# SSD exponents from one 32-row matmul per head and direction, in a hybrid SSD, MLA and GLA encoder on one core

## The reference, cut to what matters

```python
def step(state, inp):                       # ssd_scan, one chunk of 128 tokens
    xc, dtc, bc, cc = inp
    acum = jnp.cumsum(dtc * a, axis=1)
    diff = acum[:, :, None] - acum[:, None, :]
    decay = jnp.exp(jnp.where(causal, diff, -jnp.inf))
    cb = jnp.einsum('blgn,bsgn->blsg', cc, bc)
    scores = cb[..., None] * decay * dtc[:, None]
    y = jnp.einsum('blsge,bsgep->blgep', scores, xc)
    y = y + jnp.einsum('blgn,bgepn->blgep', cc, state) * jnp.exp(acum)[..., None]
    ...
y_fwd = ssd_scan(xs, dt[:, :, 0], a[0], b_in, c_in)
y_bwd = flip_seq(ssd_scan(flip_seq(xs), flip_seq(dt[:, :, 1]), a[1], flip_seq(b_in), flip_seq(c_in)))
y = y_fwd + y_bwd + xs * d_skip.astype(f32).reshape(SSD_GROUPS, SSD_HPG)[:, :, None]
```

## Time and profile before

| | |
|---|---|
| median of 3 runs | 1332.7 us (1330.87 to 1333.67) |
| the profiled execution, its own time | 1333.24 us |
| its span, first to last instruction | 1331.4 us |
| PE busy | 1316.7 us (99% of the span) |
| DVE, ACT, POOL busy | 770.4, 642.1, 624.0 us |
| mean granted clock of TensorE | 0.996 |
| input projection | to 155 us |
| SSD heads on PE behind it | 155 to 195 us |
| attention, first layer | 197 to 285 us |

### The profile page before, as it was taken

The page is one execution under the profiler, slowest core; times in us unless marked ns, Lnnn a source line. Parts: engine busy times, 40 slices in busy tenths (PEclk is TensorE's granted clock), DMA queues, the critical chain, the costliest instruction groups (busy, mean ns, idle before and its releaser), DMA issues.

```text
span 1331.4 us, 16274 instructions
## 1 busy us (share of the span) xinstructions
PE 1316.7 (99%) x6540; PEld 1112.0 (84%) x6540; DVE 770.4 (58%) x842; ACT 642.1 (48%) x1029; POOL 624.0 (47%) x294
## 2 busy tenths in 40 slices
PE   9999999999999999999999999999999999999997
PEld 7878878888898888888889988888998888888887
DVE  5857486840079998885000863436379988882002
ACT  6654777652355544444223586555555444443221
POOL 3344461245524654445553354755535644445551
PEclk9999999999999999999999999999999999999998
DMA  5342111123223333333332323311223333333331
GB/s 207 96 119 80 53 35 41 64 80 96 83 92 95 95 99 102 100 92 87 103 90 89 124 64 95 95 60 65 83 96 97 101 102 97 95 89 96 93 87 64
DMA packets 41147, 119.77 MB, mean 90 GB/s; under 512 B 4592, under 2 KB 11632, under 8 KB 41072
## 3 DMA queue, kind: packets, MB, share of 16 engines
q1 hardware_dynamic: 39712, 116.43, 28.5%
q10 hardware_dynamic: 1360, 2.29, 0.6%
HBM read 116.35 MB, written 2.23 MB: 89 GB/s over the span
## 4 chain that ended last, share of the span: by engine, by line
PE 92%; DVE 5%; ACT 1%; SPq 1%; DMA 0%; issue 0%; ACTq 0%; DVEq 0%
PE bank L345 26%; PE bank L349 26%; PE bank L348 26%; DVE sqacc L674 1%; PE bank L1819 1%; PE bank L1817 1%; PE bank L1818 1%; PE bank L2057 1%; PE bank L1370 1%; PE bank L1550 1%; PE bank L1553 1%; PE bank L398 1%; PE bank L2039 1%; PE bank L1337 1%; PE bank L1580 1%; PE bank L1339 1%
## 5 line engine op out<-in xcount | busy, mean ns | idle before, releaser
L318 POOL TENSOR_TENSOR wlo<-raw,whi 128x1024 fp32r<-128x1024 f32 (+2 forms) x214 | 530.9, 2494 | 621.5 <-ACT whi L312 621.4
L345 PE MATMUL bank<-xw_hi,whi 128*128 128x512 f32 (+1 forms) x1272 | 474.9, 374 | 1.6 <-DVE xw_lo L734 0.9
L349 PE MATMUL bank<-xw_hi,wlo 128*128 128x512 f32 (+1 forms) x1256 | 466.8, 372 | 0.0
L348 PE MATMUL bank<-xw_lo,whi 128*128 128x512 f32 (+1 forms) x1256 | 466.7, 372 | 0.0
L312 ACT ACTIVATE whi<-raw 128x1024 fp32r<-128x1024 f32 (+2 forms) x215 | 219.7, 1025 | 206.0 <-DMA raw<-in_fout 112.6
L345 PEld LDWEIGHTS bank<-xw_hi,whi 128*128 128x128 f32 x1272 | 239.7, 188 | 44.2 <-issue 2.1
L349 PEld LDWEIGHTS bank<-xw_hi,wlo 128*128 128x128 f32 x1256 | 236.5, 188 | 41.6
L348 PEld LDWEIGHTS bank<-xw_lo,whi 128*128 128x128 f32 x1256 | 236.7, 188 | 40.2 <-issue 0.2
L607 DVE RECIPROCAL small<-small 128x2 f32<-128x2 f32 x8 | 1.3, 164 | 315.2 <-ACT small L532 313.9
L760 DVE SCALAR_TENSOR_TENSOR cbuf<-ubuf,par,cbuf 128x510 f32<-128x510 f32 x100 | 168.8, 1688 | 3.5
L345 PE MATMUL bank<-g_hi,whi 128*128 128x512 f32 (+1 forms) x396 | 145.3, 367 | 0.2
(11 more groups left out here) (282 smaller groups left out, 1458.8 us busy)
## 6 DMA issues: line engine op xcount, KB each, us to landing
raw<-in_fin SPq DMA_DIRECT2D x88, 512.0 KB, 3.6
raw<-in_fout SPq DMA_DIRECT2D x32, 448.0 KB, 3.3
raw<-in_gin SPq DMA_DIRECT2D x25, 512.0 KB, 3.6
raw<-in_hin SPq DMA_DIRECT2D x22, 512.0 KB, 3.7
raw<-in_hout SPq DMA_DIRECT2D x16, 512.0 KB, 3.7
raw<-in_fout SPq DMA_DIRECT2D x16, 512.0 KB, 3.5
raw<-in_gout SPq DMA_DIRECT2D x8, 512.0 KB, 3.7
xres<-in_x SPq DMA_DIRECT2D x8, 256.0 KB, 4.6
```

Source lines behind the costliest of these rows:

```text
L318: engine.tensor_tensor(wlo[s][:, 0:n], raw[s][:, 0:n], whi[s][:, 0:n].bitcast(F32), ALU.subtract).then_inc(w_lo, 1)
L345: first = nc.tensor.matmul(out_ap, wh, ah, start=start, stop=False)
L348: nc.tensor.matmul(out_ap, wh, al, start=False, stop=False)
L349: return first, nc.tensor.matmul(out_ap, wl, ah, start=False, stop=stop)
```

## The change

The masks by -2^30 and the bias of the exponentials go away. Instead the whole exponent of a head and direction comes from one matmul over 32 rows: eight rows hold the high part of a_l of eight heads and eight the low part (`moving`, 512 columns), with ones for the head that is picked in the stationary tile, and 16 rows hold u_s, high and low, for four blocks in the stationary tile (`steady`), with ones for the block in `moving`. Rows 0 to 31 and 32 to 63 are the two directions of heads 0 to 7, rows 64 to 127 those of heads 8 to 15. The tables are made in three steps: DVE splits a_f and u_f in high and low rows (two operations more), SP writes them to DRAM (4 DMAs) and reads them back in place (16 DMAs) between the loads of blocks 10 to 14, and ACT fills the constant parts.

The two directions are joined before the exponential: DVE copies the backward exponent over the forward one where s > l (`copy_predicated`), then ACT takes one exponential of 128x512. The diagonal has the forward weight alone; the backward diagonal and the skip are a per-token coefficient (`coef`), made from sums of B times C (POOL, two products; PE, eight matmuls of one column; DVE, two small operations). POOL (chunks 0 to 3) and DVE (chunks 4 to 7) multiply x by it, token by channel, and PE adds it to the near product by four matmuls with the identity per chunk. wx[1] moves from POOL to DVE, into the first four heads. `skip` goes away. The far and near parts are summed in `reach`, so SP's next load of `reach` waits for `gated` of two chunks before, where it waited for DVE's far part.

```diff
@@ pe_spread @@
-            v = n % 2
             if first:
-                pe.wait_ge(sem("picks"), 4)
-                pe.wait_ge(sem("dt_dve"), 11)
-                pe.wait_ge(sem("at_in"), 16)
+                pe.wait_ge(sem("decays_in"), 4 * 4 * 16)
+                pe.wait_ge(sem("coef"), 1)
             else:
-                pe.wait_ge(sem("ssd_both"), n - 1)
+                pe.wait_ge(sem("ssd_exp"), n - 1)
             for d in range(2):
-                pick = ident_r[:, 32 * d + n:32 * d + n + 1].to_broadcast([P, P])
-                nc.tensor.matmul(abank(v, d)[:].rearrange("p (b x) -> p b x", b=NBLK), never_r[:, d * P:(d + 1) * P],
-                                 eye_r[:].unsqueeze(1).broadcast_to([P, NBLK, P]), start=True, stop=False)
-                nc.tensor.matmul(abank(v, d)[:], pick, at_both[:], start=False, stop=True).then_inc(sem("a_mm"), 1)
+                rows = slice(32 * (2 * (n // GHEADS) + d), 32 * (2 * (n // GHEADS) + d + 1))
+                j = n % GHEADS
+                nc.tensor.matmul(abank(n, d)[:], steady[rows, j * P:(j + 1) * P], moving[rows, :], start=True,
+                                 stop=True).then_inc(sem("a_mm"), 1)
@@ joining and exponentials @@
-        def dve_both_ways(dve, n):
-
-            dve.wait_ge(sem("ssd_exp"), EXPS * (n + 1))
-            nc.vector.tensor_tensor(ebuf[n % 4][:], ebuf[n % 4][:], abank(n, 1)[:], ALU.add).then_inc(
-                sem("ssd_both"), 1)
+        def dve_either_way(dve, n):
+
+            dve.wait_ge(sem("a_mm"), 2 * n + 2)
...
+            nc.vector.copy_predicated(fore, mask, back).then_inc(sem("ssd_way"), 1)
...
-            for b in range(NBLK):
-                at = slice(b * P, (b + 1) * P)
-                nc.scalar.activation(ebuf[n % 4][:, at], abank(n, 0)[:, at], ACT.Exp, bias=u_s(b, 0)).then_inc(
-                    sem("ssd_exp"), 1)
-            act.wait_ge(sem("a_mm"), 2 * n + 2)
-            for b in range(NBLK):
-                o = abank(n, 1)[:, b * P:(b + 1) * P]
-                nc.scalar.activation(o, o, ACT.Exp, bias=u_s(b, 1)).then_inc(sem("ssd_exp"), 1)
+            nc.scalar.activation(ebuf[n % 4][:], abank(n, 0)[:], ACT.Exp).then_inc(sem("ssd_exp"), 1)
@@ dve_ssd @@
-                nc.vector.tensor_tensor(bank[6][:], bank[6][:], reach[c % 2][:], ALU.mult).then_inc(sem("ssd_far"), 1)
-
-            def skip(c):
...
+                nc.vector.tensor_tensor(reach[c % 2][:], bank[6][:], reach[c % 2][:], ALU.mult).then_inc(
+                    sem("ssd_far"), 1)
...
                 if n + 2 < HEADS:
-                    dve_both_ways(dve, n + 2)
-                if n % 2:
-                    skip(c)
-                elif n:
+                    dve_either_way(dve, n + 2)
+                if n and n % 2 == 0:
                     gated(c - 1)
+                if n < NBLK:
+                    dve_late_x(dve, n)
@@ dve_late_x @@
+            nc.vector.tensor_tensor(by_head(wx[1], i), by_head(xtok[1], i), far_weight(i, 1), ALU.mult).then_inc(
+                sem("wx_late"), 1)
+            nc.vector.tensor_tensor(own_part(4 + i), own_x(4 + i), own_coef(4 + i), ALU.mult).then_inc(
+                sem("own_dve"), 1)
@@ y(n) of pe_ssd @@
+                if u == 0:
+                    pe.wait_ge(sem("own_dve" if c >= 4 else "own_pool"), c % 4 + 1)
+                    for b in range(NBLK):
+                        at = slice(b * P, (b + 1) * P)
+                        nc.tensor.matmul(bank[4 + c % 2][:, at], ck(xbc, c)[:, at], ident[:], start=b == 0,
+                                         stop=False)
@@ pe_own_sums, behind block 20 @@
+            for b in range(NBLK):
+                for g in range(2):
+                    last = nc.tensor.matmul(bank[2][:, 2 * b + g:2 * b + g + 1], ebuf[2 + g][:, b * P:(b + 1) * P],
+                                            ones[:, 0:1], start=True, stop=True)
@@ dve_dt @@
+            step(nc.vector.tensor_copy(rows_of[2][:], u_f))
+            done(13)
+            step(nc.vector.tensor_tensor(rows_of[3][:], u_f, rows_of[2][:].bitcast(F32), ALU.subtract))
@@ block.sync @@
+                if f == BASE["hin"] + 10:
+                    sp_decays_out(sp)
+                if 0 <= f - BASE["hin"] - 11 < 4:
+                    sp_decays_in(sp, f - BASE["hin"] - 11)
@@ sp_reach @@
             if c >= 2:
-                sp.wait_ge(sem("ssd_far"), c - 1)
+                sp.wait_ge(sem("ssd_y"), 2 * c - 2)
```

More of the change, by code:

```diff
@@ L194, in build_program @@
             ebuf = [sb(f"ebuf{i}", T, F32, s) for i in range(4)]
+            with ExitStack() as q:
+                rows_of = [sb(f"rows{i}", T, F32R, q, 64) for i in range(4)]
             cbm = sb("cbm", 4 * T, F32, s)
-            at_both = sb("at_both", T, F32R, s)
-            at_lo = sb("at_lo", T, F32R, s, 64)
+            moving = sb("moving", T, F32R, s)
             reach = [sb(f"reach{i}", T, F32, s) for i in range(2)]
             gt = sb("gt", T, F32, s, 64)
-            ident_r = sb("ident_r", 64, F32R, s)
-            eye_r = sb("eye_r", P, F32R, s)
-            never_r = sb("never_r", 2 * P, F32R, s)
             cols = sb("cols", NBLK * 2 * 64, F32, s)
+            steady = sb("steady", GHEADS * P, F32R, s)
+            coef = sb("coef", NBLK * HEADS, F32, s)
         with ExitStack() as s:
@@ L990, in pool_hin @@
                 los(pool, at)
+                if at == BASE["hin"] + TURN0:
+                    pool_b_times_c(pool)
             pool.wait_ge(sem("cb_set"), NBLK)
+            for c in range(KD // 2):
+                pool_own(pool, c)
             pool_mask(pool, 0)
@@ L1109, in pe_dt_turn @@
             for b in range(NBLK):
-                for w, src in enumerate((w_f, u_f)):
+                for w, src in enumerate((w_f, dt_f)):
                     last = nc.tensor.transpose(bank[2][:, b * P + w * 64:b * P + w * 64 + 64],
@@ new lines, in pe_own_sums, with dve_coefs @@
+        def pe_own_sums(pe):
+            pe.wait_ge(sem("b_times_c"), 2)
+            pe.wait_ge(sem("dt_dve"), 15)
+            for b in range(NBLK):
+                for g in range(2):
+                    last = nc.tensor.matmul(bank[2][:, 2 * b + g:2 * b + g + 1], ebuf[2 + g][:, b * P:(b + 1) * P],
+                                            ones[:, 0:1], start=True, stop=True)
+            last.then_inc(sem("own_sums"), 1)
+        def dve_coefs(dve):
+            dve.wait_ge(sem("own_sums"), 1)
+            backward = cols[:].rearrange("p (b x) -> p b x", b=NBLK)[:, :, 96:96 + HEADS]
+            nc.vector.tensor_tensor(coef[:].rearrange("p (b g n) -> p b g n", b=NBLK, g=2),
+                                    backward.rearrange("p b (g n) -> p b g n", g=2),
+                                    bank[2][:, 0:2 * NBLK].rearrange("p (b g) -> p b g", b=NBLK).unsqueeze(3).broadcast_to(
+                                        [P, NBLK, 2, GHEADS]), ALU.mult).then_inc(sem("coef"), 1)
+            dve.wait_ge(sem("coef"), 1)
+            every = coef[:].rearrange("p (b n) -> p b n", b=NBLK)
+            nc.vector.tensor_tensor(every, every, con("skips", HEADS).unsqueeze(1).broadcast_to([P, NBLK, HEADS]),
+                                    ALU.add).then_inc(sem("coef"), 1)
@@ L1204, in abank @@
             return bank[2 * (1 - n % 2) + d]
-        def dve_both_ways(dve, n):
-            dve.wait_ge(sem("ssd_exp"), EXPS * (n + 1))
-            nc.vector.tensor_tensor(ebuf[n % 4][:], ebuf[n % 4][:], abank(n, 1)[:], ALU.add).then_inc(
-                sem("ssd_both"), 1)
+        def dve_either_way(dve, n):
+            dve.wait_ge(sem("a_mm"), 2 * n + 2)
+            mask = con("later").bitcast(mybir.dt.uint32).unsqueeze(1).broadcast_to([P, NBLK, P])
+            fore, back = (abank(n, d)[:].rearrange("p (b l) -> p b l", b=NBLK) for d in range(2))
+            nc.vector.copy_predicated(fore, mask, back).then_inc(sem("ssd_way"), 1)
         def dve_ssd(dve):
@@ L2493 @@
     cst, rope, glac = _constants()
+    cst[:, CCOLS["skips"]:CCOLS["skips"] + HEADS] = np.asarray(inputs["ssd_d"])[0]
     data |= {"cst": cst, "rope": rope, "glac": glac}
```

127 lines of the change are left out of this document (79 added, 48 removed).

## The result

The changed kernel takes 1334.17 us (median of 20 runs, 1333.19 to 1335.80); the kernel before, run beside it on the same chip, 1331.80 (20 runs, 1330.03 to 1334.22). The ratio is 1.0017, 95% interval 1.0011 to 1.0024: 2.3 us slower, 1.5 to 3.2. That is the "no difference" of the forecast, which drew its line at 0.2%, and 0.7 from its 1333.5. But the forecast had set a change of +0.8 on a median of 1332.7 from three runs; over 20 runs that median is 1331.8, and the change +2.4. So 1.6 us of the change are to be explained, and the hit in the number is partly luck.

A forecast was written before the change was run, and what follows sets the result against it. PE's own list of work bounds the kernel, with ACT, DVE and POOL following. Terms summed to +0.8 on the profiled 1333.24, giving 1334.0, or 1333.5 us as the median; range 1329.8 to 1337.8, one in ten on each side.

The forecast's parts named there:

- no difference: Whole kernel: time within 0.2% (2.7 us) of the kernel before; chance 0.54.
- spreads, with the shape changes: SSD heads on PE: two matmuls for four in 16 heads, -9.3, and 12 changes of array shape, +1.8.
- identity matmuls: SSD chunks on PE: four float32 matmuls of 128 columns per chunk, not hidden, 8 x 0.87 = +7.0.
- sums of B times C: PE's list: eight matmuls of one column with the start of the next block, +1.8; POOL's and DVE's parts hidden.
- block 11: Block 11 starts late through two new DVE operations in the table chain, +0.9 (ends 0 and 2.0).
- wait at head 5: Start of the heads: PE waits for head 3's exponential, behind head 2's joining, exponential and ACT's table loads; +1.8.
- clock behind it: Rival: the clock falls in the new wait at head 5, the stage pays up to 1.6, 1335.1; chance 0.08.
- end of the stage: End of the heads: PE's idle time of 1.97 shrinks to 0 to 0.45, -1.6.
- clock at `rope(0)`: Half clock at 197 to 200 us behind the 1.97 idle goes with PE busy up to `rope(0)`, -1.6.
- no overlap: Rival: the two directions' spread matmuls do not overlap, as shape changes could drain the array; +1.9, 1335.4; chance 0.13.
- DVE's backlog: First two chunks: DVE needs 5.6 against PE's 5.0, largely inside PE's wait; 0.3 at most, not booked.
- the DVE rival: Rival: joining of 1.2 to 1.4 makes DVE hold PE in the first two chunks, 1336.7 or 1338; chance 0.17.

The follow-up runs named there:

- the last experiment: The kernel with three repairs (ACT's detour, DVE's late operations, decay rows moved), with B times C taken from the diagonal of cbm; 1328.73 us, ratio to the kernel before 0.9976.
- the joining twice: The changed kernel with each head's copy_predicated done twice, the second waiting for the first; 1338.73 us in its one run.
- the detour moved: The changed kernel with block 22's silu, the next high part and both ACT table loads ahead of head 2's exponential; 1332.46 us, ratio to the kernel before 1.0006.
- load 10: The changed kernel with SP's load of block 10 ahead of the decay-row writes, and the reads one load later; 1333.87 us, ratio 1.0011.

## Why the forecast was right or wrong

Each term beside what the traces show. "Measured" is the shift between the same PE instructions in the two profiled executions, or the piece itself.

| step | forecast | measured | from |
|---|---|---|---|
| spreads, with the shape changes | -7.5 | -8.7 | heads 0 to 3 0.39 each, the others 0.6 (1.19 per chunk) |
| identity matmuls | +7.0 | +7.1 | 8 x 0.89 |
| sums of B times C | +1.8 | +1.8 | 1.68 and 0.11 at the next block's start; 1.83 in the last experiment |
| block 11 | +0.9 | +1.4 | wait 1.17, and a first matmul of 0.47 |
| wait at head 5 | +1.8 | +1.8 | 1.81 |
| clock behind it | rival, 0.08 | +1.6 | only in some executions; it covers 0.7 of DVE's backlog |
| end of the stage | -1.6 | -1.6 | 1.97 to 0.38 |
| closing sums | 0 | -0.1 | before, L1385 waited 0.13 for DVE's L1221 |
| clock at `rope(0)` | -1.6 | -1.5 | in one of the two executions of the kernel before |
| sum | +0.8 | +1.8 | up to `rope(0)` |
| outside the span | 0 | +0.3 | 2.1 in each of 20 runs, 1.8 before |

**The mechanisms** came out nearly all as said: PE's list sets the time, the eight identity matmuls are not hidden, the exponentials that ACT lost are worth nothing, the wait at head 5 has the cause, place and length that were worked out, and a joining of double length has the price that its rival gave it.

**The spread** is the term that was mis-sized. I took the middle between side by side and one after the other, 0.34 for a pair, from the near products, whose overlap in columns is partial. The pair in different rows overlaps entirely: 0.23, beside the 0.20 of its change of shape. The changes of shape were sized too low in turn, 0.15 each where the chain shows 0.20. So 16 x (0.92 - 0.23) is -11.0 for the -9.3, and 12 x 0.20 is +2.4 for the +1.8. The forecast had named the Trainium skill, TensorE: Matmul & The Clock Gate, Part 3; the trace agrees with it (4 ns, and 0.23 less per pair than in one row group). With the other page of the Trainium skill that it had named, TensorEngine Tiling (Array Packing), Key Properties, the traces agree as far as a change costs something, and the price stands beside the overlap, not in its place: 0.20 for the change back to 128 rows. The rival "no overlap" fell. With the pair and the changes right the sum would have been about -0.3, further from the +2.4 of the medians: this error and the next ones partly hid each other.

**Block 11** was named with its causes and sized too low. DVE's two operations cost the 1.0 that was worked out. SP's order, whose cover the forecast called thin, cost 0.2, and the first matmul behind the wait 0.2.

**The clock** was a wrong kind of term. I read a half clock behind one idle time in one execution as its consequence, and booked 1.6 for its going. It is a chance, in the kernel before as in the new one, and the new wait has one too (four of six traces). Booking the one in full and leaving the other as a rival of 0.08 put the forecast 1.6 low against these two executions. How often each falls over many runs isn't known.

**DVE's backlog** at the start was put at 0.3 at most and not booked. It is 0.73 where the clock stays up. The step that failed: I let the backlog lie in PE's wait, but two operations that read two SBUF tiles waited out a POOL mask each there (timelines of the changed kernel):

```profile
163.97 1.75 DVE L1263 TENSOR_TENSOR wx<-xtok,cols 128x512 f32<-128x512 f32 x1
165.64 1.75 DVE L1265 TENSOR_TENSOR xbc<-xtok,coef 128x512 f32<-128x512 f32 x1
163.62 3.23 POOL L1202 TENSOR_TENSOR ebuf<-ebuf,cbm 128x512 f32<-128x512 f32 x2
```

Each started just behind a mask (163.62 and 165.13) and ended 0.55 behind its end (165.17 and 166.85).

**The joining** "has no row" is wrong: the kernel before has COPY_PREDICATED in its second layer, which I had passed over, in the groups of DVE:

```profile
L2206 DVE COPY_PREDICATED att<-tri,bank 128x256 f32<-128x256 uint32 x8 | 3.1, 442 | 3.5 <-PE bank L2039 3.5
```

442 ns for 256 columns. The new one takes 686 for 512. With that row the DVE rival would not have held 0.17.

**Outside the span** 0.3 us were added in every run. What makes them isn't settled; no run was made for it. The kernel with the joining twice had 1.8 again, and the last kernel 1.9 to 2.05.

What is left open: up to `rope(0)` the two executions are accounted for, +1.8. By the end of the span +0.5 of it is left, since the changed kernel's start was 0.3 earlier and this execution of the kernel before lost 1.0 further on, as told above. Its second execution did not. Held against that one, the terms without the clock at `rope(0)` make +3.3, the start takes off 0.3, and the spans differ by 3.0 (1331.95 and 1328.95): the account closes to the end. The medians differ by 2.4. The two pairs of executions, with the 0.3 outside the span, give 0.8 and 3.3, so the median lies between them. That its place there is a matter of how often the clock falls in either kernel is argued, not shown.

## What to carry to other kernels

Price a matmul of few rows by what stands beside it: here the second one, in another row group, added nothing that the chain shows, but a change back to all rows costs what the overlap saves, so put such matmuls together and not one pair between two full ones. Count what an engine does between two operations before you make the second depend on a third engine: a detour that cost nothing (ACT's table loads) became the bound as soon as the operation ahead of it had to wait, and moving it into the gap that the new wait opens gave it back. Before a term of the clock is booked, look whether a second execution has it.

## What the runs showed of the hardware

- Two float32r matmuls over 32 rows and 512 columns in neighbouring row groups, into different banks, start 4 ns apart and last 0.43 together with the change from a 64-column matmul; in one row group they start 0.33 apart and last 0.66. The far product over 128 rows that follows takes 1.09, behind a spread over 128 rows 0.89.
- Whether the granted clock falls to 1.2 GHz behind a short idle time of TensorE is not decided by its length: it fell behind 0.9 (the detour moved) and 1.97 (the kernel before) and stayed at 2.4 GHz behind 1.81 (load 10) and behind the same 1.97 (the kernel before again). A fall cost 1.4 to 1.6. Behind the wait at head 5 it fell in four of six traces.
- COPY_PREDICATED of 128x512 float32 from PSUM to PSUM with a mask from SBUF took 0.69, and 0.60 from start to start, as the TENSOR_TENSOR operations of 128x512 around it.
- A DVE operation on SBUF tiles alone that started while a POOL operation ran ended 0.55 us behind the end of that one: in the changed kernel at 163.02 (1.03 us), 163.97 and 165.64 (1.75 each), 194.33 (1.38) and 198.34 (1.77), where they take 0.69 and 0.74 alone. The other way round, with DVE 0.03 us ahead in the last kernel, POOL's took 1.85 for 1.26. (A DVE operation that started 0.02 us before the POOL operation's end, at 160.54, kept its 0.69.) The far parts and joinings beside a POOL operation, which read PSUM, stayed at 0.68 to 0.69.
